# First norm of a diffusion block booked by row block, adaLN sums dealt by columns, and the q weights moved under the next stage's first weights

## The reference

```
h = h + 0.5 * gate0 * swiglu(norm_modulate(h, norm_ffn1, shift0, scale0), w_ffn1_in, w_ffn1_out)
h = h + gate1 * mix(norm_modulate(h, norm_mix, shift1, scale1), ...)     # pooling mixer || windowed attention
h = h + 0.5 * gate2 * swiglu(norm_modulate(h, norm_ffn2, shift2, scale2), w_ffn2_in, w_ffn2_out)
norm_modulate(x, g, shift, scale) = rmsnorm(x, g) * (1 + scale) + shift
mod = silu(c) @ w_mod[l] + b_mod[l]      # adaLN: 9 vectors of 1024 per layer, for c and for c_ctx
```

## Time and profile before

| | |
|---|---|
| median of 3 runs | 2875.01 us (2874.98 to 2948.72) |
| profiled execution | 2869.1 us, span 2867.3 us (slowest core, core 3) |
| spans of the 8 cores | 2858.6, 2866.4, 2843.1, 2867.3, 2847.9, 2864.1, 2857.8, 2866.5 us |
| granted PE clock | 0.974 to 0.980 of full speed |
| PE busy | 2656.3 us (93%) |
| DVE, ACT, POOL busy | 1197.9 (42%), 809.7 (28%), 306.5 us (11%) |

### The profile page before, as it was taken

The page is one execution under the profiler, slowest core; times in us unless marked ns, Lnnn a source line. Parts: engine busy times, 40 slices in busy tenths (PEclk is TensorE's granted clock), DMA queues, the critical chain, the costliest instruction groups (busy, mean ns, idle before and its releaser), DMA issues.

```text
span 2867.3 us, 47036 instructions; the slowest of 8 cores (2843.1 to 2867.3 us)
## 1 busy us (share of the span) xinstructions
PE 2656.3 (93%) x15952; PEld 1374.6 (48%) x15952; DVE 1197.9 (42%) x2592; ACT 809.7 (28%) x1294; POOL 306.5 (11%) x428
## 2 busy tenths in 40 slices
PE   3899999998887799999899999999998878999998
PEld 1455555554443355554445555555544444444445
DVE  1465356524555566436653222222245553112124
ACT  3311321113454411221123112211235542122122
POOL 3000000002212100000000000000022121000000
PEclk9999999999999899999999999999999989999999
DMA  9455346641000367336734341334520004425453
GB/s 212 121 143 129 70 116 149 151 86 40 16 9 1 80 163 166 95 74 161 170 87 76 65 80 31 68 67 80 102 53 16 7 1 74 86 54 89 74 111 118
DMA packets 94435, 250.09 MB, mean 87 GB/s; under 512 B 11264, under 2 KB 19200, under 8 KB 93440
## 3 DMA queue, kind: packets, MB, share of 16 engines
q0 software_dynamic: 42464, 153.76, 30.5%
q1 hardware_dynamic: 51744, 93.34, 10.2%
HBM read 392.42 MB, written 8.39 MB: 140 GB/s over the span
## 4 chain that ended last, share of the span: by engine, by line
PE 82%; DMA 6%; DVE 5%; issue 3%; ACT 3%; POOL 0%; SPq 0%; DVEq 0%; ACTq 0%; POOLq 0%
PE ps L125 72%; PE ps L123 10%; DMA arena<-wmod 5%; ACT arena L796 1%; DVE arena L416 1%; DVE arena L494 1%; DMA arena<-xT 1%; DMA arena<-wab 1%; DVE arena L698 1%; ACT arena L503 0%; POOL arena L453 0%; ACT arena L716 0%; DVE arena L823 0%; DVE arena L600 0%; DVE arena L717 0%
## 5 line engine op out<-in xcount | busy, mean ns | idle before, releaser
L125 PE MATMUL ps<-arena 128*128 128x512 bf16 (+5 forms) x13933 | 2513.2, 328 | 155.3 <-ACT arena L796 42.8
L125 PEld LDWEIGHTS ps<-arena 128*128 128x128 bf16 x13933 | 1213.3, 99 | 1271.1 <-issue 262.0
L123 PE MATMUL ps<-arena 128*128 128x512 bf16 (+6 forms) x2019 | 637.7, 345 | 49.0 <-ACT arena L450 30.1
L600 DVE TENSOR_TENSOR arena<-arena,ps 128x512 bf16<-128x512 f32 (+2 forms) x484 | 290.9, 601 | 723.8 <-PE ps L123 682.1
L598 ACT ACTIVATE arena<-ps 128x512 f32<-128x512 f32 (+2 forms) x484 | 256.2, 529 | 1151.7 <-PE ps L123 1061.6
L548 DVE SCALAR_TENSOR_TENSOR arena<-ps,arena 128x512 f32<-128x512 f32 (+3 forms) x296 | 176.9, 608 | 556.3 <-PE ps L123 556.0
L416 DVE SCALAR_TENSOR_TENSOR arena<-arena 128x512 f32<-128x512 f32 x512 | 352.7, 689 | 114.2 <-DMA arena<-wmod 86.3
L123 PEld LDWEIGHTS ps<-arena 128*128 128x128 bf16 (+1 forms) x2019 | 194.8, 99 | 214.7 <-issue 78.4
L503 ACT ACTIVATE arena<-arena 128x512 bf16<-128x512 f32 (+3 forms) x256 | 179.5, 725 | 281.8 <-DVE arena L494 212.3
L143 POOL DMA_DIRECT2D arena<-wab x176 | 93.4, 535 | 1269.3 <-PE ps L123 1254.0
L796 ACT ACTIVATE arena<-ps 128x1024 bf16<-128x1024 f32 x167 | 161.4, 1028 | 52.0 <-PE ps L123 36.3
(11 more groups left out here) (39 smaller groups left out, 224.1 us busy)
## 6 DMA issues: line engine op xcount, KB each, us to landing
arena<-wab POOLq DMA_DIRECT2D x176, 512.0 KB, 6.3
arena<-wmod SPq DMA_DIRECT2D x256, 256.0 KB, 4.6
arena<-wo POOLq DMA_DIRECT2D x64, 704.0 KB, 7.8
outT<-arena SPq DMA_DIRECT2D x26, 256.0 KB, 3.3
arena<-xT SPq DMA_DIRECT2D x8, 640.0 KB, 21.2
arena<-wmod POOLq DMA_DIRECT2D x16, 256.0 KB, 21.7
arena<-xT SPq DMA_DIRECT2D x16, 256.0 KB, 12.8
arena<-wout POOLq DMA_DIRECT2D x4, 1024.0 KB, 11.1
```

Of the source, the lines that this page charges most:

```text
L123: self.ops["pe"].append(lambda e, l=l, r=r, o_i=o_i, st_i=st_i, sp_i=sp_i: e.matmul(o_i, l, r, start=st_i, stop=sp_i, skip_group_check=sha ...
L125: self.ops["pe"].append(lambda e, l=l, r=r, o_i=o_i, st_i=st_i, sp_i=sp_i: e.matmul(o_i, l, r, start=st_i, stop=sp_i, skip_group_check=sha ...
L600: S.op("dve", lambda e: e.tensor_tensor(gTb[:, j, off:off + n], sa_s[pi][:, 0:n], pb[pi][:, 0:n], ALU.mult), reads=[("sa", pi), BK[2 + pi] ...
```

## The change

It has four parts.

1. The first norm's shift and scale get one key per row block (`("mod0", k)`), `mod_first` takes two DVE instructions in place of three (a constant `bm1` is formed once), and the sums of squares on PE alternate with `first_mm` of four row blocks as their chunks land.
2. The list `late` is dealt by unit: (1,0), (1,1), (1,2), (2,0), (2,1), (2,2), (1,3), (2,3), then tile 0. `x` columns 1280 on are asked for before `cB`.
3. The adaLN tasks are dealt by columns: a unit gets a share in proportion to its width, and none is dealt at `j` = 19 and 20, nor at the first two `j` of ffn2. 16 tasks of layer 1 move from ffn2 to ffn1: now 128 tasks in each. `c_rows` becomes the first of ffn2's tasks.
4. `wq` moves under `wab` slots 0 and 1, `pooled` and `aot` under slots 2 and 3, and `pre_load` asks for the first two `wab` of ffn2 at the start of t = 5.

```diff
@@ mix arena
         wkvu = alloc(BF16, [8, WKV], dma=True, key=("wkvu",))
+        wq = alloc(BF16, [8, 512], dma=True, key=("wq",))
         pooled = parts(BF16, [4, 512], "pooled")
         aot = parts(BF16, [4, 512], "aot")
...
-        wq = alloc(BF16, [8, 512], dma=True, key=("wq",))
@@ norm_steps
+            def mod_keys(k):
+                if (par, i_norm) == (0, 0):
+                    return [("mod0", k)]
+                return [("modraw", par, shift_i), ("Amod", par, i_norm)]
@@ ffn
+        def pre_load(l, f):
+            for j in range(2):
+                pre_in[l, f, j] = j
+                S.dma("pool", None, wab_s[j], wab[l, f, j].rearrange("p (a k c) -> p a k c", a=2, k=8), writes=[("wab", j)])
+            cnt["ab"] = 2
...
-            nslots = sum(NJ * len(subtiles(n)) for _, n in segs) - (NWAB * len(late) if late else 0)
-            done = [0]
+            def share(si, j, n):
+
+                if j in (NJ - 3, NJ - 2) or (si == 0 and j < (NWAB if late else 2)):
+                    return 0
+                return n
+
+            nshare = sum(share(si, j, n) for si, (_, n) in enumerate(segs) for j in range(NJ))
+            done = [0, 0]
...
-                        for ex in extra[done[0] * len(extra) // nslots:(done[0] + 1) * len(extra) // nslots]:
-                            ex()
-                        done[0] += 1
+                        done[0] += share(si, j, n)
+                        while done[1] < len(extra) * done[0] // nshare:
+                            extra[done[1]]()
+                            done[1] += 1
@@ mix
                 if t == 5:
+                    pre_load(l, 1)
                     side = tail()
@@ mod_first
-                 reads=[BK[c % 4], ("bm", 0)], writes=[("modraw", 0, 0)])
-            S.op("dve", lambda e: e.tensor_scalar(A0, scl, bm[:, 8 + c:9 + c], 1.0, ALU.add, ALU.add),
-                 reads=[BK[c % 4], ("bm", 0)], writes=[("Amod", 0, 0)])
-            S.op("dve", lambda e: e.tensor_scalar(A0, A0, gn_l[0][:, 0, c:c + 1], None, ALU.mult),
-                 reads=[("Amod", 0, 0), ("gn", 0)], writes=[("Amod", 0, 0)])
+                 reads=[BK[c % 4], ("bm", 0)], writes=[("mod0", c)])
+            S.op("dve", lambda e: e.tensor_scalar(A0, scl, modraw_l[0][:, 8 + c, 0:1], gn_l[0][:, 0, c:c + 1], ALU.add, ALU.mult),
+                 reads=[BK[c % 4], ("bm1",), ("gn", 0)], writes=[("mod0", c)])
@@ l0_first
-            x_load(1024, 256, after=[chunks[15][0]])
+            x_load(1024, 256, after=[("wab", 0)])
             x_load(0, 512, after=[("wab", 1)])
+            x_load(1280, 1280, after=[("wab", 3)])
             c_load()
-            x_load(1280, 1280, after=[("wab", 3)])
-            for c in range(8):
+            def first_mod(c):
                 first_mm(c, chunks)
                 mod_first(c)
+            for k in range(9):
+                first[1][k]()
+                if k in (0, 2, 4, 5):
+                    first_mod((0, 2, 4, 5).index(k))
+            for c in range(4):
                 first[2][c]()
-            late = [(1, {0: norms[2][0], 1: norms[2][1], 2: norms[2][2] + norms[0][0], 3: norms[0][1]}),
-                    (2, {0: norms[0][2][0:3], 1: norms[0][2][3:6], 2: norms[0][2][6:8]}), (0, {})]
-            extra = mod_tasks(0, [2, 4, 3, 5, 7, 6, 8])
+            for c in range(4, 8):
+                first_mod(c)
+                first[2][c]()
+            late = [(1, 0, norms[2][0]), (1, 1, norms[2][1] + norms[2][2] + norms[0][0]), (1, 2, []), (2, 0, []),
+                    (2, 1, norms[0][1] + norms[0][2][0:4]), (2, 2, norms[0][2][4:8]), (1, 3, []), (2, 3, [])]
+            late += [(0, j, []) for j in range(4)]
+            extra = mod_tasks([(0, m) for m in (2, 4, 3, 5, 7, 6, 8)] + [(1, 0)])
@@ l0_ffn2
-            mod_load(1)
             c_load()
-            c_rows()
-            extra = mod_tasks(1, list(range(9))) + [lambda i=i: mod_derive(1, i) for i in range(3)]
+            extra = [c_rows] + mod_tasks([(1, m) for m in range(1, 9)]) + [lambda i=i: mod_derive(1, i) for i in range(3)]
```

More of the change, by code:

```diff
@@ L397, in mod_derive, with mod_tasks @@
             mod_gate(l, i)
-        def mod_tasks(l, ms):
-            par = l % 2
-            parts_ = [(8 * m + c, h) for m in ms for c in range(8) for h in range(2)]
+        def mod_tasks(ms):
+            parts_ = [(l, 8 * m + c, h) for l, m in ms for c in range(8) for h in range(2)]
             held = {}
             def load(n):
-                idx, h = parts_[n]
+                l, idx, h = parts_[n]
                 i = held[n] = cnt["wm"] % NWM
@@ L411, in sums @@
             def sums(n):
-                idx, h = parts_[n]
+                l, idx, h = parts_[n]
+                par = l % 2
                 i, m, c = held.pop(n), idx // 8, idx % 8
@@ L500, in mod_step @@
                             dst(k, off, m), tmp[:, off:off + m], Amod[:, i_norm, k, 1:2], modraw[:, shift_i * 8 + k, 1:2], ALU.mult, ALU.add),
-                            reads=[("tmp", ti), ("modraw", par, shift_i), ("Amod", par, i_norm)], writes=dst_keys(k))
+                            reads=[("tmp", ti)] + mod_keys(k), writes=dst_keys(k))
                         continue
@@ L606, in ffn @@
                     slots = [in_load(j) for j in range(first)]
-                    for sti, after in late:
-                        off, n = sts[sti]
-                        for j in range(first):
-                            in_step(j, slots[j], sti, off, n)
-                            for st in after.get(j, ()):
-                                st()
+                    for sti, j, after in late:
+                        in_step(j, slots[j], sti, *sts[sti])
+                        for st in after:
+                            st()
                     cnt["ab"] = 0
@@ L1002, in l0_first @@
             first = norm_steps(512, 512, 0, lambda k, o2, m: nTb[:, k, 512 + o2:512 + o2 + m], lambda k: [("nT", k, 1)], early=True)
-            for fs in first[:2]:
-                for f in fs:
-                    f()
+            for f in first[0]:
+                f()
+            mod_load(1)
             chunks = {}
@@ L1013, in l0_first @@
             cnt["ab"] = NWAB
-            x_load(1024, 256, after=[chunks[15][0]])
+            x_load(1024, 256, after=[("wab", 0)])
             x_load(0, 512, after=[("wab", 1)])
+            x_load(1280, 1280, after=[("wab", 3)])
             c_load()
-            x_load(1280, 1280, after=[("wab", 3)])
-            for c in range(8):
+            S.op("dve", lambda e: e.tensor_scalar(modraw_l[0][:, 8:16, 0], bm_l[0][:, 8:16], 1.0, None, ALU.add),
+                 reads=[("bm", 0)], writes=[("bm1",)])
+            def first_mod(c):
                 first_mm(c, chunks)
                 mod_first(c)
-                first[2][c]()
-            late = [(1, {0: norms[2][0], 1: norms[2][1], 2: norms[2][2] + norms[0][0], 3: norms[0][1]}),
-                    (2, {0: norms[0][2][0:3], 1: norms[0][2][3:6], 2: norms[0][2][6:8]}), (0, {})]
-            extra = mod_tasks(0, [2, 4, 3, 5, 7, 6, 8])
+            for k in range(9):
[3 more added lines that the diff above has]
+            for c in range(4):
+                first[2][c]()
+            for c in range(4, 8):
[5 more added lines that the diff above has]
+            extra = mod_tasks([(0, m) for m in (2, 4, 3, 5, 7, 6, 8)] + [(1, 0)])
             extra[15:16] = [extra[15], lambda: mod_gate(0, 0)]
```

## The result

The changed kernel takes 2884.1 us in the median of 13 executions, against 2876.9 us of the kernel before on the same chip. So it is a little slower, by 0.3%, where 0.7% faster was forecast. It lies inside the range of 2826 to 2890 and inside 2%, but on the other side of no change. The profiled execution has a span of 2878.7 us on core 4, the slowest; the mean of the spans of all cores went from 2859.0 to 2870.3 us.

The account below looks back on a forecast made before the run. Matmuls were 82% of the last-ending chain, so only PE's waits could be won. Start -7, passages -12.5 and -8, dealing +7 sum to -20.5: 2869.1 - 20.5 + 5.9 = 2854.5 us, range 2826 to 2890.

Parts of the forecast that it names:

- Dealing, +7: Layer 0's ffn1 and ffn2: adaLN tasks packed into fewer `j` lose 37 us against 29.9 before, +7 us.
- The price of 1.07 per `j`: ffn2's second segment, layer 0: time lost per `j` before the change, 1.07 us; 0.7 taken for after it.
- twice the shortest landing, 5.4 us, inside the room of 5.8: `wmod` loads beside POOL's queue: by the turn-taking rule they land in time, making the dealing term about -25.
- rival (a): ffn1 and ffn2: the dealing pays in full, DVE's waits staying inside PE's slack; term -25, 2822.5 us, chance 0.20.
- Rival (b): Layer 0's ffn1 and ffn2: three `wmod` buffers bind at every `j`; term +49, 2896.5 us, chance 0.15.
- Start, -7: Kernel start up to tile 0: scalings right behind an rstd up to 3 us sooner, tile 0 earlier, -7 us.
- Mix to ffn2, layer 0, -12.5: Passage in layer 0: early `wab` loads remove PE's 10.70 us pause and the slow first `j`, -12.5 us.
- Mix to ffn2, layer 1, -8: Passage in layer 1: unit (0,0) starts at once, the next waits for the late norm, -8 us.

Follow-up runs that it names:

- e15: Changed kernel with five `wmod` buffers, `j` = 17 and 18 free of tasks, tile 0's sums before unit (2,0): 2821.7 us, 0.9834 of the kernel before.
- e1: Changed kernel with the adaLN tasks dealt as in the kernel before, new start and early `wab` loads kept: ratio 0.9943 to the kernel before.
- e3: Kernel before with only the early `wab` loads, the moved `wq` buffer and the later SiLU of the `c` rows: 14.4 us gained.

## Why the prediction was wrong

**Dealing, +7; measured +25.6. This is the step that failed, as a size.** The mechanism was named and is right: three loads under way, a task period of 2.43 us, DVE waits that PE has to share. What was wrong is the even spreading over the `j`. I took 0.35 us per `j` over 54 `j` (19), 0.7 in 20 `j` (14) and 4 more, 37 lost, against 29.9 lost before. Measured against e15, which loses nothing, the changed kernel loses 15.7 in the `j` up to 17, 18.5 in the four `j` = 18, and 15.2 in the stretches behind them, 49.4; and the kernel before 23.8. So the loss per ordinary `j` was estimated too high, and two thirds of the real loss stood in a place to which the sum gave no term. Of the added loss, 7 us lie in the `j` up to 17, 12 in the four `j` = 18 and 7 behind them; that the first of these equals my +7 is luck, for of the 37 and 29.9 that I subtracted only 15.7 and 8.5 lie there. The price of 1.07 per `j` in ffn2's second segment, on which the 29.9 and the 0.7 rest, was that of core 3; the mean over the cores was 0.63, before the change and after it. The row for the missing place was there: the landing of 14.5 us in the earlier trace rows belongs to just this place, and I used it only to turn down a rule. The change puts its free `j` directly behind the collision, and so makes the tasks before it denser.

On that rule: the Trainium skill (DMA: Bandwidth & Descriptors, Queues, rings and completion order) says that an engine takes turns between the queues with work, packet by packet. I had turned it into "twice the shortest landing, 5.4 us, inside the room of 5.8". Beside `wab` and `wo` the loads took 9.2 us in the median, where they took 4.6 otherwise; that is twice, as taking turns would have it, but twice the usual landing and not the shortest. These three loads do not contradict the rule, nor do they show that it is the cause; what I drew from it for rival (a) was drawn wrongly. Rival (b), the ring as the bound, had the right cause and stood at 2896.5; its even price per `j` was wrong for the same reason as mine.

**Start, -7; measured +1 to +2.** The first half of the step held: the first FFN matmul at 45.69 instead of 51.77. The failing half is "the rstd comes up to 3 sooner, because unit (1,3) no longer stands before its sums". Two other units stand before them now, and one waits for tile 2; the rstd came at 81.41 instead of 78.35, and the pauses of PE moved and did not go. The other 4.2 us of this term, from the rstd to tile 0, came only in part: 13.6 us after the change, 15.3 before. I had looked at what left the queue ahead of the sums and not at what took its place.

**Mix to ffn2, layer 0, -12.5; measured -13.2 after the change, -11.2 in e1 and e3.** The mechanism is right: no wait for `wab`, and no slow clock behind it. But 1.98 us of pause are left where the sum allowed 0.6, so that it is a little luck that the number fits so well.

**Mix to ffn2, layer 1, -8; measured -3.3 after the change and -6.1 in e3.** The pause of 2.58 us and the direct start of unit (0,0) are as forecast. From the end of the mix to the end of the first `j` it takes 10.4 us in the mean over the cores where it took 16.5, so the passage itself gives 6.1. The 8.1 of the forecast were those of core 3, which took 17.7 before. The lower clock behind the pause, the 1 to 2 us that were named, comes on one core of the changed kernel (its first `j` takes 12.05 us, the others 10.36) and on seven of e3. The rest is the longer mix of layer 1 on some cores, which is open.

## What to carry to other kernels

Waiting time of a prefetch ring should be laid out by place, not divided by the number of steps: look for the one step at which another large transfer goes out, and keep the ring's consumers away from that step or move the transfer. Here a step left free helped only where it was the one with the transfer; behind it, it only made the others denser. And when an order is rewritten, ask of every instruction that is moved what stands ahead of it now, in each in-order queue, not only what no longer does.

## What the runs showed of the hardware

- The price of more tasks on the same ring is steep: with loads that land in 4.6 us and three buffers, 3.20 tasks per 8.65 us cost 0.2 us in 17 `j`, 3.56 cost 3.5 and 4.00 cost 11.6.
- One stop costs more than its length: a stop of PE of 6.5 us was followed by matmuls at the lower clock (3.15 us for seven), and the stretch that begins at the end of `j` = 18 and holds this stop was 8.8 us longer on this core than in e15, so about 2.3 us on top of the stop. Most of a loss is still the stop itself: in the changed kernel 25 of the 34 us at and behind `j` = 18 are time in which PE stands.
- Three loads of 256 KB landed in 9.2 us in the median beside a 512 KB and a 704 KB load of another queue, and fifty others in 4.6.
